# Feature-layout blocks of a two-layer network kernel: order of the two kinds of matrix products

## The reference

```python
u = rms_norm(x) @ w_in                        # 6,096 columns, SSD and RWKV inputs
x = x + concat(y_ssd, y_rwkv) @ w_out
q, k, v = h @ wq, m @ wk, m @ wv              # cross attention, then @ wo
x = x + square(relu(h @ ffn_w1)) @ ffn_w2     # 2048 -> 8192 -> 2048
proj = h @ w_in_2                             # 7,176 columns
x = x + concat(o_a, o_b) @ w_out_2
x = x + (silu(conv(h @ w_gate)) * (h @ w_up)) @ w_down   # 2048 -> 5632 -> 2048
return rmsnorm(x, final_gain)
```

## Time and profile before

| | |
|---|---|
| time, median of 3 runs | 2782.42 us (2781.78 to 2784.34) |
| profiled execution: span, first to last instruction | 2783.1 us |
| profiled execution: time beside the span | not given; its span lies within the three runs |
| PE busy | 2752.2 us, 99% |
| DVE busy | 1728.2 us, 62% |
| ACT busy | 1341.1 us, 48% |
| mean granted TensorE clock | 0.998 |
| moved by DMA | 506.70 MB, 182 GB/s |

### The profile page before, as it was taken

One profiled execution on the slowest core, in us unless ns is written; L12 is line 12 of the kernel. 1 busy time (PEld: TensorE's weight loads), 2 busy tenths in 40 slices (PEclk: granted clock), 3 DMA queues, 4 the chain that ended last, 5 costly groups with the idle time before them and its releaser, 6 DMA issues.

```text
span 2783.1 us, 41120 instructions
## 1 busy us (share of the span) xinstructions
PE 2752.2 (99%) x17279; PEld 2349.8 (84%) x17279; DVE 1728.2 (62%) x2049; ACT 1341.1 (48%) x1717; POOL 39.7 (1%) x63
## 2 busy tenths in 40 slices
PE   8999999999999999999999999999999999999998
PEld 7888888888888888888888888888888888888887
DVE  5787668654655555556556666556666756765675
ACT  6745435544555444434444555545554444443444
POOL 1000000000000000000000100000000000000001
PEclk9999999999999999999999999999999999999999
DMA  7565227556455656656565555555555555555553
GB/s 236 165 206 190 94 75 248 180 192 195 159 167 182 195 189 190 194 188 192 194 186 195 182 182 195 169 166 171 177 182 189 190 196 185 183 195 195 193 185 136
DMA packets 395317, 506.70 MB, mean 182 GB/s; under 512 B 11441, under 2 KB 287422, under 8 KB 394366
## 3 DMA queue, kind: packets, MB, share of 16 engines
q1 hardware_dynamic: 380925, 488.26, 54.3%
q10 hardware_dynamic: 14208, 15.81, 1.8%
HBM read 501.87 MB, written 2.17 MB: 181 GB/s over the span
## 4 chain that ended last, share of the span: by engine, by line
PE 96%; DVE 2%; ACT 1%; issue 1%; DMA 0%; ACTq 0%; SPq 0%; DVEq 0%
PE PS L694 39%; PE PS L699 33%; PE PS L703 16%; PE PS L952 3%; PE PS L742 1%; PE PS L1182 0%; PE PS L1162 0%; PE PS L725 0%; DVE wlo L2199 0%; DMA slab<-in_x 0%; PE PS L1131 0%; PE PS L890 0%; ACT whi L1511 0%; ACT slab L1565 0%; PE PS L853 0%
## 5 line engine op out<-in xcount | busy, mean ns | idle before, releaser
L2199 DVE TENSOR_TENSOR wlo<-raw,whi 128x1024 fp32r<-128x1024 f32 x922 | 1128.4, 1229 | 782.9 <-ACT whi L1511 778.8
L1511 ACT ACTIVATE whi<-raw 128x1024 fp32r<-128x1024 f32 x922 | 971.8, 1058 | 930.7 <-PE PS L694 458.7
L699 PE MATMUL PS<-XX,whi 128*128 128x512 f32 (+1 forms) x3856 | 1216.5, 397 | 1.5 <-DVE wlo L2199 1.2
L703 PEld LDWEIGHTS PS<-XX,wlo 128*128 128x128 f32 (+1 forms) x3856 | 724.6, 188 | 171.4
L703 PE MATMUL PS<-XX,wlo 128*128 128x256 f32 (+1 forms) x3856 | 759.9, 278 | 0.0
L699 PEld LDWEIGHTS PS<-XX,whi 128*128 128x128 f32 (+1 forms) x3856 | 589.1, 189 | 5.8 <-issue 2.3
L694 PE MATMUL PS<-whi,act 128*128 128x512 f32 x2208 | 593.1, 390 | 0.0
L694 PEld LDWEIGHTS PS<-whi,act 128*128 128x128 f32 x2208 | 411.8, 188 | 83.9
L694 PE MATMUL PS<-wlo,act 128*128 128x512 f32 x1104 | 340.1, 389 | 0.0
L694 PE MATMUL PS<-whi,XX 128*128 128x512 f32 x1024 | 280.8, 396 | 3.9 <-ACT slab L1525 2.1
L694 PEld LDWEIGHTS PS<-wlo,act 128*128 128x128 f32 x1104 | 207.3, 188 | 43.4
(11 more groups left out here) (415 smaller groups left out, 1355.6 us busy)
## 6 DMA issues: line engine op xcount, KB each, us to landing
raw<-in_ffn_w SPq DMA_DIRECT2D x128, 1024.0 KB, 5.4
raw<-in_w_in SPq DMA_DIRECT2D x103, 1024.0 KB, 5.1
raw<-in_w_ffn_gate SPq DMA_DIRECT2D x44, 1024.0 KB, 4.8
raw<-in_w_ffn_up SPq DMA_DIRECT2D x44, 1024.0 KB, 4.9
raw<-in_w_ffn_down SPq DMA_DIRECT2D x44, 1024.0 KB, 5.1
raw<-in_w_out SPq DMA_DIRECT2D x32, 1024.0 KB, 5.1
raw<-in_xattn_wk SPq DMA_DIRECT2D x16, 1024.0 KB, 5.3
raw<-in_xattn_wv SPq DMA_DIRECT2D x16, 1024.0 KB, 5.1
```

The lines of the kernel that those rows point to most:

```text
L699: T.matmul(ps[0:wd, f, :], whi[:, o:o + wd], b.x[:, kk, :], start=first, stop=False, skip_group_check=True)
L703: mm = T.matmul(ps[0:wd, f, 0:SEQ], wlo[:, o:o + wd], b.x[:, kk, 0:SEQ], start=False, stop=last, skip_group_check=True)
L1511: S.activation(k.whi[:, h % 4, 0:b.size], k.raw[:, t % 4, u * b.size:(u + 1) * b.size], ACT.Copy).then_inc(k.w_hi, 1)
L2199: V.tensor_tensor(k.wlo[:, h % 4, 0:b.size], k.raw[:, h // 2 % 4, u * b.size:(u + 1) * b.size], k.whi[:, h % 4, 0:b.size].bitcast(F32), AL ...
```

## The change

In feature layout the order of the products of a k-tile changes. Before, both groups' 512-column products come first and then both groups' 256-column products: f0 rounded, f1 rounded, f0 remainder, f1 remainder. After, each group's 256-column product follows directly its own 512-column product: f0 rounded, f0 remainder, f1 rounded, f1 remainder. To this end parts is cut into two generators, tok_half with the token layout as it was, and feat_half. The slices, the flags, the place of the yield and the increment of w_used are the same as before, and so are all other engines' programs.

```diff
--- before.py
+++ after.py
@@ -681,31 +681,45 @@
             if h == b.last - 3:
                 self.by_tokens(b, h)
             return
+        if b.mode == "tok":
+            yield from self.tok_half(b, q, u, h, ps)
+        else:
+            yield from self.feat_half(b, q, u, h, ps)
+
+    def tok_half(self, b, q, u, h, ps):
+        k = self.k
+        T = k.nc.tensor
         for a in range(b.kpt // 2):
             kk = b.kpt * q + b.kpt // 2 * u + a
             if b.there is not None:
                 T.wait_ge(*b.there(kk))
-            first, last = kk == 0, kk == b.kt - 1
             w = slice(a * b.ncol, a * b.ncol + b.ncol)
             whi, wlo = k.whi[:, h % 4, w], k.wlo[:, h % 4, w]
-            if b.mode == "tok":
-                for m, (wt, lo) in enumerate(((whi, 0), (whi, SEQ), (wlo, 0))):
-                    for tt in range(NT):
-                        mm = T.matmul(ps[:, tt, :], b.x[:, kk, lo + tt * P:lo + (tt + 1) * P], wt,
-                                      start=first and m == 0, stop=last and m == 2)
-            else:
-                for f, wd in enumerate(b.widths):
-                    o = sum(b.widths[:f])
-                    T.matmul(ps[0:wd, f, :], whi[:, o:o + wd], b.x[:, kk, :], start=first, stop=False,
-                             skip_group_check=True)
-                for f, wd in enumerate(b.widths):
-                    o = sum(b.widths[:f])
-                    mm = T.matmul(ps[0:wd, f, 0:SEQ], wlo[:, o:o + wd], b.x[:, kk, 0:SEQ], start=False, stop=last,
-                                  skip_group_check=True)
+            for m, (wt, lo) in enumerate(((whi, 0), (whi, SEQ), (wlo, 0))):
+                for tt in range(NT):
+                    mm = T.matmul(ps[:, tt, :], b.x[:, kk, lo + tt * P:lo + (tt + 1) * P], wt,
+                                  start=kk == 0 and m == 0, stop=kk == b.kt - 1 and m == 2)
             if a == b.kpt // 4 - 1:
                 yield
         mm.then_inc(k.w_used, 1)
 
+    def feat_half(self, b, q, u, h, ps):
+
+        k = self.k
+        T, n = k.nc.tensor, b.kpt // 2
+        for a in range(n):
+            kk = b.kpt * q + n * u + a
+            if b.there is not None:
+                T.wait_ge(*b.there(kk))
+            for f, wd in enumerate(b.widths):
+                o = a * b.ncol + sum(b.widths[:f])
+                T.matmul(ps[0:wd, f, :], k.whi[:, h % 4, o:o + wd], b.x[:, kk, :], start=kk == 0, stop=False,
+                         skip_group_check=True)
+                mm = T.matmul(ps[0:wd, f, 0:SEQ], k.wlo[:, h % 4, o:o + wd], b.x[:, kk, 0:SEQ], start=False,
+                              stop=kk == b.kt - 1, skip_group_check=True)
+            if a == n // 2 - 1:
+                yield
+        mm.then_inc(k.w_used, 1)
 
     def by_tokens(self, b, first):
```

## The result

| | before | after |
|---|---|---|
| median | 2782.75 us (2781.78 to 2784.34, 5 runs) | 2797.68 us (2793.63 to 2798.78, 5 runs) |
| span of the profiled execution | 2783.1 us | 2797.5 us |

The ratio is 1.0047, with a 95% interval of 1.0036 to 1.0057: the change makes the kernel 0.47% slower, where 0.23% faster was forecast (6.3 us). The time lies above the forecast range, which ended at 2784.0, and beyond even the slower rival's 2789.2.

A forecast was written before the change was run, and what follows sets the result against it. Taken as bound by the spacing of products on PE: 2048 x 3.3 ns = 6.8 us gained, 0.5 us of it lost early, so -6.3 us from the 2782.42 us median to 2776.1 us; range 2774.0 to 2784.0.

The forecast's parts named there:

- What bounds the kernel: Products queued on PE, busy 99% of the span; feature-block time is number of products times spacing of starts.
- The counts: Feature blocks: the change reorders 2048 groups of four products (quads: two of 512, two of 256 columns), adding and removing none.
- today's 696.7 ns: Time of four feature products in the old order, from 15 such groups in the timeline before.
- I take 3.3 ns as the gain per quad: Feature blocks: each four reordered products were to take 693.4 instead of 696.7 ns, 6.8 us over 2048.
- narrow block: Feature block with one group and 16 k-tiles, already alternating 512 and 256 columns before: 346.9 ns a pair.
- finer reading: Token blocks' 13.36 ns over the columns, applied to every feature product: 693.4 ns for four.
- Rival D: The slower rival, feature blocks: switching bank from a 256-column to a 512-column product costs 3.3 ns; 2789.2 us, chance 0.10.
- B: Rival, feature blocks: the extra goes with bank switches, four become two, half the gain; 2779.2 us, chance 0.13.
- C: Rival, feature blocks: order does not matter, today's extra belongs to the layout and stays; 2782.4 us, chance 0.14.
- E: Rival, feature blocks: short products between long ones go at 117.9 ns, 689 ns for four; 2767.5 us, chance 0.06.
- Token blocks unchanged: Check: products in token blocks should stay at 226.7 ns each, else the prediction would be wrong.
- No wait: Check: PE's idle before the feature products should not rise above 2.7 us, else a wait replaced the spacing.

The follow-up runs named there:

- Experiments 2: Changed kernel, but each half takes all k-tiles of group 0 first, then all of group 1, so the bank switches once: 2796.74 us, ratio 1.0046.
- 4: Changed kernel, but bank switches from long to short product and stays from short to long, except in each block's first k-tile: 2797.17 us, ratio 1.0047.
- experiment 12: Changed kernel, with weight loads of 64 instead of 128 columns from each block's second k-tile on: 2753.91 us, one timed run.
- 15: Order of the kernel before, with weight loads of 64 columns as in experiment 12: 2785.82 us, one timed run.
- experiment 13: Kernel of 9, with the old-order k-tile moved from first to second block of each long run, keys as they were: 2780.46 us, ratio 0.9994.
- 9: Old order except in long runs, which alternate; those expected slow get one old-order k-tile at their start: 2792.23 us, ratio 1.0034.
- experiment 14: As experiment 13, but the six runs are entered through one whole old-order block and alternate from their second block: 2778.91 us, ratio 0.9987.
- 17: As experiment 14, with the first two blocks of w_in_2 in the old order too: 2777.61 us against 2782.11, ratio 0.9983.
- experiment 1: The changed kernel run and profiled once more, unedited: 2794.98 us, one timed run.
- experiments 5: Changed kernel, with the first k-tile of each half in the old order: 2787.00 us, ratio 1.0013.
- 6: Changed kernel, with only the first k-tile of each block in the old order: 2788.67 us, ratio 1.0023.
- experiments 8: Changed kernel, with one more product of 128 columns ahead of each feature block that follows a token block: 2798.67 us, ratio 1.0057.
- experiments 10: Changed kernel, with the remainder's product lengthened from 256 to 384 columns: 3027.83 us, one timed run.
- 11: Order of the kernel before, with the remainder's product lengthened from 256 to 384 columns: 3044.86 us, one timed run.

## Why the prediction was wrong, point by point

- **What bounds the kernel**: right. The span follows the spacing of starts on PE and nothing else; no other engine entered.
- **The counts** (2048 quads) and **today's 696.7 ns**: right, and reproduced wherever the old order was kept.
- **The step that failed** is "I take 3.3 ns as the gain per quad". The price behind it, 346.7 ns a pair, was measured rightly in the narrow block and occurs, by the starts of the trace, in a fifth of the changed products (about 1600 of 8192). What was wrong is that it was taken for a property of the order. It is one of two spacings of that order, and most of the long runs got the other: +10.0 ns a quad instead of -3.3. The narrow block was a single sample of how such a run can be entered. The "finer reading" by 13.36 ns for each product of the token blocks agreed with it and made it look like a law; agreement of two numbers for one side said nothing of a second side. The short product in L1162 at 117.9 ns, which broke that law, was on the table.
- **Rival D** forecast the right sign, with a wrong cause and less than half of the size. Experiments 2 and 4 removed or moved its switches and the time stayed at 1.0046 and 1.0047. B, which also counts switches, falls with it. C falls with the change itself: quads of 693.3 and 706.7 ns where the old order has 696.7, and a ratio whose interval excludes 1. With half loads order alone is worth 32 us (12 beside 15, one run each). E's 689 ns was never seen with full loads.
- **Token blocks unchanged** at 226.7 ns: right (382 products from 1159.78 us in 86.60 us in the chain after).
- **No wait**: right.
- **The gap of the Trainium skill** (TensorE: Matmul & The Clock Gate, Back-to-back issue gap), N/2.4 + 2.5 ns, is below every spacing of feature and token products here and knows no second one. It gives 215.8 ns for 512 columns in a row, where 226.7 was measured, and, as an estimate from it, 325.0 ns for a pair, where 346.7 and 353.3 were. The same section's statement that weight loads take part in the spacing agrees with experiment 12.

That the long spacing makes nearly all of the loss is shown by the sums over the trace (13.2 of 14.4 us in feature products), by experiment 13 beside 9 (the same products, 11.8 us apart), and by 14 and 17: with it gone from the long runs, the alternation gains what the prediction said of a quad. In 9, 13, 14 and 17 the short runs between small products have the old order throughout, so these kernels say nothing of them; and what lies behind small products moves by as much from execution to execution (+1.4 us in the profiled one, -1.9 in experiment 1, both against the kernel before). What decides the side at an entry is shown only in part. A k-tile in the old order turns a running rhythm over (experiments 5, 6 and 13, in every long run); at the start of a run it changed one run of seven (9), and an added short product none (8); a settled block in the old order led to the short spacing in all seven long runs entered that way (six in 14, w_in_2 too in 17). The same program can take either side at one place (experiment 1). Why there are two, and what in the engine holds the state over hundreds of products, stays open. Banks, buffers, clock, supply and, by experiments 10 and 11, too short a cover for the load are excluded; the width of the load and unequal lengths take part.

## What to carry to other kernels

When the rate of a stream of products is read off one place of a trace, look how many separate entries into that stream it rests on: a rate can have two stable values with the same instructions. Reordering products of unequal length on a saturated TensorE cost up to 0.6% and gained up to 0.2% here (experiments 8 and 17), and must be measured run by run over the whole trace, not by its mean. If an alternating order is wanted, check each long run's spacing, and enter it through a different order where it is the long one; the check has to be repeated after any edit, since experiment 14 turned a run that it had not touched.

## What the runs showed of the hardware

- A stream of alternating products of 512 and 256 columns runs at 346.7 or at 353.3 ns a pair at the same granted clock, and stays there for up to 1024 products; at one place two executions of the same program had one each (experiment 1).
- Over one period the time above the columns was a multiple of 3.33 ns within the reading in each settled stream listed here: 53.3, 56.7 and 66.7 ns for four products of 512 and 256 columns, 40.0 and 60.0 with half loads, 123.3 ns for eight in groups of four (701.7 x 2 - 1280), 13.3 ns for one of 512.
- Making the shorter product longer, 384 instead of 256 columns, raised the time above the columns from 13.3 or 16.7 to 16.7 or 20.0 ns a product.
- Loads of 64 columns instead of 128 lowered it to 10.0 ns in the alternating order and raised it from 14.2 to 15.0 ns in the old one.
